# A gated delta-rule scan: the running inverse held as two stacked 64-row blocks, and decay sums turned from columns

## What is computed

```python
G = jnp.cumsum(g, axis=-1)
gamma = jnp.exp(jnp.where(incl, G[..., :, None] - G[..., None, :], -jnp.inf))
kb = k * beta[..., None]
a_low = jnp.where(strict, jnp.einsum('bhnid,bhnjd->bhnij', kb, k) * gamma, 0.0)
rhs = jnp.concatenate([v * beta[..., None], kb * jnp.exp(G)[..., None]], axis=-1)
uw = lax.linalg.triangular_solve(eye + a_low, rhs, left_side=True, lower=True, unit_diagonal=True)
qk = jnp.einsum('bhnid,bhnjd->bhnij', q, k) * gamma
...
v_new = u_n - jnp.einsum('bhck,bhkv->bhcv', w_n, s)
o_n = jnp.einsum('bhck,bhkv->bhcv', qd_n, s) + jnp.einsum('bhij,bhjv->bhiv', qk_n, v_new)
s = s * jnp.exp(gl_n)[..., None, None] + jnp.einsum('bhck,bhcv->bhkv', kd_n, v_new)
```

## Time and profile before

| | us |
|---|---|
| median of three runs | 4089.0 |
| the profiled execution's own time | 4089.51 |
| its span, first to last instruction | 4087.7 |
| TensorE matmuls busy | 3717.2 (91% of the span) |
| VectorE busy | 2009.5 (49%) |
| ScalarE busy | 910.1 (22%) |
| POOL busy | 461.1 (11%) |

### The profile page before, as it was taken

How to read it: one execution, slowest core, us unless ns; L and a number is a source line. 1 busy time by engine, 2 the same in 40 slices (tenths; PEclk the granted TensorE clock), 3 DMA queues, 4 the chain that set the end, 5 groups by cost and what they waited for, 6 DMA issues and landing times.

```text
span 4087.7 us, 54482 instructions
## 1 busy us (share of the span) xinstructions
PE 3717.2 (91%) x22980; PEld 3063.8 (75%) x22980; DVE 2009.5 (49%) x2777; ACT 910.1 (22%) x1583; POOL 461.1 (11%) x374
## 2 busy tenths in 40 slices
PE   5989999989899999898989899899999789979996
PEld 3777777767777777687878787788887667658885
DVE  3445333544453335575656566542234552765346
ACT  1114100221141001234433442110011201721011
POOL 0001000000010000004620562030000010512000
PEclk9878999988789999898999999999999989989998
DMA  3210344322103443210001003111111211012222
GB/s 131 88 56 1 142 171 178 115 94 83 52 1 142 165 171 127 108 42 13 2 27 42 13 2 122 57 55 71 63 62 62 90 62 62 1 42 93 93 93 83
DMA packets 48615, 314.44 MB, mean 77 GB/s; under 512 B 5836, under 2 KB 6732, under 8 KB 13944
## 3 DMA queue, kind: packets, MB, share of 16 engines
q1 hardware_dynamic: 37440, 272.65, 18.2%
q10 hardware_dynamic: 10936, 38.31, 2.5%
HBM read 301.38 MB, written 9.56 MB: 76 GB/s over the span
## 4 chain that ended last, share of the span: by engine, by line
PE 79%; DVE 8%; DMA 6%; issue 2%; ACT 2%; PEld 2%; POOL 1%; POOLq 0%; ACTq 0%; PEldq 0%; DVEq 0%; SPq 0%; another core or an unknown queue 0%
PE psum L511 19%; PE psum L512 18%; PE psum L513 18%; DMA pieces_in<-pieces 5%; PE psum L2072 3%; PE psum L2082 3%; PE psum L2070 2%; DVE pieces_lo L536 1%; PE psum L1127 1%; PE psum L917 1%; PE psum L1100 1%; PE psum L2902 1%; PE psum L1111 1%; PE psum L2924 1%; PE psum L1432 1%
## 5 line engine op out<-in xcount | busy, mean ns | idle before, releaser
L511 PE MATMUL psum<-xt_operands,pieces_hi 128*128 128x512 f32 (+1 forms) x2544 | 946.5, 372 | 31.0 <-DVE pieces_lo L536 26.2
L512 PE MATMUL psum<-xt_operands,pieces_hi 128*128 128x512 f32 (+1 forms) x2544 | 929.4, 365 | 0.0
L513 PE MATMUL psum<-xt_operands,pieces_lo 128*128 128x512 f32 (+1 forms) x2544 | 928.8, 365 | 0.0
L511 PEld LDWEIGHTS psum<-xt_operands,pieces_hi 128*128 128x128 f32 x2544 | 481.9, 189 | 149.5 <-issue 44.6
L529 DVE CAST pieces_hi<-pieces_in 128x2048 fp32r<-128x2048 f32 x206 | 257.3, 1249 | 576.5 <-DMA pieces_in<-pieces 490.9
L513 PEld LDWEIGHTS psum<-xt_operands,pieces_lo 128*128 128x128 f32 x2544 | 481.5, 189 | 77.8
L512 PEld LDWEIGHTS psum<-xt_operands,pieces_hi 128*128 128x128 f32 x2544 | 482.3, 190 | 75.3 <-issue 2.4
L536 DVE TENSOR_TENSOR pieces_lo<-pieces_in,pieces_hi 128x2048 fp32r<-128x2048 f32 x206 | 480.2, 2331 | 5.7
L511 PE MATMUL psum<-pieces_hi,xt_operands 128*128 128x512 f32 (+1 forms) x1000 | 403.8, 404 | 30.1 <-DVE pieces_lo L536 17.8
L512 PE MATMUL psum<-pieces_lo,xt_operands 128*128 128x512 f32 (+1 forms) x1000 | 390.8, 391 | 0.0
L513 PE MATMUL psum<-pieces_hi,xt_operands 128*128 128x512 f32 (+1 forms) x1000 | 390.7, 391 | 0.0
(11 more groups left out here) (323 smaller groups left out, 4843.2 us busy)
## 6 DMA issues: line engine op xcount, KB each, us to landing
pieces_in<-pieces SPq DMA_DIRECT2D x260, 1024.0 KB, 4.8
arena<-mods ACTq DMA_DIRECT2D x8, 512.0 KB, 14.2
arena<-ln ACTq DMA_DIRECT2D x4, 1024.0 KB, 4.8
x_park<-x_mem ACTq DMA_DIRECT2D x1, 3072.0 KB, 11.4
o_park<-arena ACTq DMA_DIRECT2D x2, 1536.0 KB, 5.4
arena<-o_park ACTq DMA_DIRECT2D x1, 3072.0 KB
x_mem<-x_park ACTq DMA_DIRECT2D x1, 3072.0 KB, 18.0
arena<-line ACTq DMA_DIRECT2D x6, 448.0 KB, 5.9
```

What stands on the lines that cost most here:

```text
L511: signal_later(k, pe.matmul(out, sh, mh, start=start, stop=False))
L512: signal_later(k, pe.matmul(out, sh, ml, start=False, stop=False))
L513: return pe.matmul(out, sl, mh, start=False, stop=stop)
```

## The change

X is no longer a 128 x 128 tile. While the inverse is built in blocks of 64 and less, only its two diagonal 64 x 64 blocks are not zero, and these are now stacked: `xc` is 128 x 64 for each head, rows 0 to 63 the upper block and rows 64 to 127 the lower one. A product with a block-diagonal stationary of 128 x 128 and `xc` as moving operand gives both blocks at once, in 64 columns (`thin`). Such a result takes 256 columns of a bank (`compact`), and VectorE adds and ScalarE copies of these are 128 x 256. The first X now comes from TensorE (`xp`, `ld` turned by a product with a stacked identity) and VectorE (`x1`). `w0` and `w1` turn the blocks by eight 64 x 64 products with an identity, `w2` by four. `v1a` places the finished blocks in a full tile `xf`, by two additions; `xf` is cleared once before the scan. `gb` becomes a transpose of the running sums, which the stage before has already put into columns (`PRE`). `ORDERS` and the loops are written out anew, and `IN_BLOCKS` names five operations, so that 10 operations of a turn use the one ring and 44 the other.

```diff
-IN_BLOCKS = ("l2", "u2", "x2", "l4", "u4", "x4", "l8", "x8", "y0", "xx0", "y1", "xx1")
+IN_BLOCKS = ("l2", "l4", "l8", "w0", "w1")
...
-def x_of(k, s, d):
-    return k.buf[d][f"x{s % 2}"]
+def compact(k, name, s, d):
+    return k.ps[:, PLACE[name, s, d][0], 0:256].rearrange("p (h c) -> p h c", c=64)
...
+    def thin(s, d, name, lhs, rhs, *needs):
 
         if not runs(s):
             return
         ready(s, d, name, needs)
-        rows, columns = halves(d)
         for h in range(HALF):
-            last = pe.matmul(bank(k, name, s, d)[rows, h, columns], lhs(s, d, h)[lhs_rows, rows],
-                             rhs(s, d, h)[lhs_rows, columns], start=True, stop=True)
+            last = pe.matmul(compact(k, name, s, d)[:, h, :], lhs(s, d, h), rhs(s, d, h), start=True, stop=True)
         st.done(last)
...
+    def turned_blocks(s, d, name, *needs):
...
+        for h in range(HALF):
+            for r in BLOCKS:
+                last = pe.matmul(bank(k, name, s, d)[r, h, r], k.buf[d]["xc"][r, h, :], k.ident[r, r], start=True, stop=True)
+        st.done(last)
...
-    def log_decay(s, d, h):
-        return g[:, CHUNKS[d][s], 4 * d + h:4 * d + h + 1].broadcast_to([P, P])
+    def prefixes(s, d, h):
+        return prefix[:, CHUNKS[d][s], 4 * d + h:4 * d + h + 1].broadcast_to([P, P])
...
     def gb(s, d):
-        product(s, d, "gb", log_decay, lambda s, d, h: tri[:, d, :])
+        product(s, d, "gb", prefixes, None)
...
+    def xp(s, d):
+        thin(s, d, "xp", b("ld"), lambda s, d, h: eye)
...
     def x2(s, d):
-        blocks(s, d, "x2", b("l2"), x, "x1")
+        thin(s, d, "x2", b("l2"), b("xc"), "x1")
...
     def w0(s, d):
-        product(s, d, "w0", x, None, "x8a")
+        turned_blocks(s, d, "w0", "x8a")
...
     def y0(s, d):
-        blocks(s, d, "y0", b("lv"), x, "lv0", "x8a")
+        thin(s, d, "y0", b("lv"), b("xc"), "lv0")
...
     def xx0(s, d):
-        blocks(s, d, "xx0", b("u2"), b("l2"), "w0c", "y0c")
+        thin(s, d, "xx0", b("u2"), b("yc"), "y0c")
...
     for d in range(2):
         e.link(dve.memset(k.state[d], 0.0))
+        e.link(dve.memset(k.buf[d]["xf"], 0.0))
...
     def v1a(s, d):
-        x = x_of(k, s, d)
-        tt(s, d, "v1a", x, ps("xx1", s, d), x, ALU.add, "xx1")
+        if runs(s):
+            st.begin("v1a", s, d, ("xx1",))
+            for r in BLOCKS:
+                ins = dve.tensor_tensor(k.buf[d]["xf"][r, :, r], compact(k, "xx1", s, d)[r, :, :],
+                                        k.buf[d]["xc"][r, :, :], ALU.add)
+            st.done(ins)
...
-    def x1(s, d):
-        tt(s, d, "x1", x_of(k, s, d), k.buf[d]["ud"], heads(k.ident), ALU.add, "ud")
```

More of the change, by code:

```diff
@@ L1538, in place2 @@
             k.buf[d][n] = room.take(HALF, P)
+        for n in ("xc", "yc"):
+            room = b if b.at + 256 <= b.end else b2 if b2.at + 256 <= b2.end else b3
+            k.buf[d][n] = room.take(HALF, 64)
     a = Arena(arena, 0, work_end)
@@ L1954 @@
 ORDERS = {
[L1955 to L1965, removed]
+    "pe": order("x4.0' l2.1' l8.0' u2.1' ks.1' x8.0' l4.1' w0.0' x2.1' y0.0' u4.1' x4.1' xx0.0' l8.1' y1.0' w1.0' "
+      "x8.1' gb.0 xx1.0' w0.1' y0.1' o1.0' xx0.1' w2.0' y2.0' w1.1' y1.1' xx2.0' gb.1 xx1.1' vn.0' o1.1' "
+      "w2.1' y2.1' o2.0' xx2.1' su.0' vn.1' kk.0 o2.1' qk.1 qk.0 kk.1 ut.0 xp.0 l2.0 ks.0 u2.0 su.1' l4.0 "
+      "x2.0 ut.1 xp.1 u4.0 "),
+    "dve": order("x2a.0' x4a.0' x1.1' x8a.0' r1.1' x2a.1' rr.1' x4a.1' v0a.0' x8a.1' diff.0 v1a.0' rr.0' v0a.1' t1.0' "
+      "s1.0' v2a.0' diff.1 v1a.1' t1.1' s1.1' v2a.1' t2.0' dlow.0 s2.0' low0.0 low.0 t2.1' qg.1 dlow.1 qg.0 "
+      "low0.1 low.1 r1.0 x1.0 s2.1' "),
+    "act": order("y1c.0' w1c.0' w0c.1' y0c.1' w2c.0' y2c.0' w1c.1' y1c.1' vnc.0' w2c.1' y2c.1' vnc.1' gam.0 gamt.0 "
+      "gamt.1 ud.0 gam.1 l2c.0 u2c.0 l4c.0 ud.1 u4c.0 l2c.1 l8c.0 u2c.1 l4c.1 w0c.0 y0c.0 u4c.1 l8c.1 "),
+    "pool": order("lv1.1' lv2.1' dup.0 kd.1' bv.1 dup.1 ld.0 oa.0' kd.0 oa.1' ld.1 lv0.0 lv0.1 lv1.0 bv.0 lv2.0 "),
 }
@@ L2080, in blocks @@
         for h in range(HALF):
-            for r in (slice(0, 64), slice(64, P)):
+            for r in BLOCKS:
                 last = pe.matmul(bank(k, name, s, d)[r, h, r], lhs(s, d, h)[r, r], rhs(s, d, h)[r, r],
                                  start=True, stop=True)
+        st.done(last)
+    def thin(s, d, name, lhs, rhs, *needs):
+        if not runs(s):
+            return
+        ready(s, d, name, needs)
+        for h in range(HALF):
+            last = pe.matmul(compact(k, name, s, d)[:, h, :], lhs(s, d, h), rhs(s, d, h), start=True, stop=True)
+        st.done(last)
+    def turned_blocks(s, d, name, *needs):
+        if not runs(s):
+            return
+        ready(s, d, name, needs)
+        for h in range(HALF):
+            for r in BLOCKS:
+                last = pe.matmul(bank(k, name, s, d)[r, h, r], k.buf[d]["xc"][r, h, :], k.ident[r, r], start=True, stop=True)
         st.done(last)
@@ L2139, in x4 @@
     def x4(s, d):
-        blocks(s, d, "x4", b("ld"), x, "x2a")
+        thin(s, d, "x4", b("ld"), b("xc"), "x2a")
     def l8(s, d):
@@ L2145, in x8 @@
     def x8(s, d):
-        blocks(s, d, "x8", b("l2"), x, "l8c", "x4a")
+        thin(s, d, "x8", b("l2"), b("xc"), "l8c")
     def w0(s, d):
-        product(s, d, "w0", x, None, "x8a")
+        turned_blocks(s, d, "w0", "x8a")
     def w1(s, d):
-        product(s, d, "w1", x, None, "v0a")
+        turned_blocks(s, d, "w1", "v0a")
     def w2(s, d):
-        product(s, d, "w2", x, None, "v1a")
+        if not runs(s):
+            return
+        ready(s, d, "w2", ("v1a",))
+        rows, _ = halves(d)
+        for h in range(HALF):
+            last = pe.matmul(bank(k, "w2", s, d)[rows, h, rows], k.buf[d]["xf"][rows, h, rows], k.ident[rows, rows],
+                             start=True, stop=True)
+        st.done(last)
     def y0(s, d):
-        blocks(s, d, "y0", b("lv"), x, "lv0", "x8a")
+        thin(s, d, "y0", b("lv"), b("xc"), "lv0")
     def y1(s, d):
-        blocks(s, d, "y1", b("lv"), x, "lv1", "v0a")
+        thin(s, d, "y1", b("lv"), b("xc"), "lv1", "v0a")
     def y2(s, d):
-        corner(s, d, "y2", b("lv"), halves(d)[1], x, "lv2")
+        corner(s, d, "y2", b("lv"), halves(d)[1], own_block, "lv2")
     def xx0(s, d):
-        blocks(s, d, "xx0", b("u2"), b("l2"), "w0c", "y0c")
+        thin(s, d, "xx0", b("u2"), b("yc"), "y0c")
     def xx1(s, d):
-        blocks(s, d, "xx1", b("u2"), b("l2"), "w1c", "y1c")
+        thin(s, d, "xx1", b("u2"), b("yc"), "w1c", "y1c")
     def xx2(s, d):
-        corner(s, d, "xx2", b("u2"), halves(d)[0], b("l2"), "w2c", "y2c")
+        corner(s, d, "xx2", b("u2"), halves(d)[0], b("yc"), "y2c")
     def ks(s, d):
@@ L2178, in vn @@
     def vn(s, d):
-        product(s, d, "vn", x, b("rr"), "v2a")
+        product(s, d, "vn", b("xf"), b("rr"), "v2a")
     def o1(s, d):
@@ L2237, in l8c, with thin_copy @@
         copy(s, d, "l8c", "l2", "l8", "l8")
+    def thin_copy(s, d, name, src, *needs):
+        if runs(s):
+            apply(s, d, name, "yc", compact(k, src, s, d), ACT.Copy, 1.0, *needs)
     def w0c(s, d):
@@ L2242, in y0c @@
     def y0c(s, d):
-        copy(s, d, "y0c", "l2", "y0", "y0")
+        thin_copy(s, d, "y0c", "y0", "y0")
     def w1c(s, d):
@@ L2299, in ps, with thin @@
         return bank(k, name, s, d) if runs(s) else None
+    def thin(name, s, d):
+        return compact(k, name, s, d) if runs(s) else None
     def col(i, s, d):
@@ L2345, in v2a @@
             st.begin("v2a", s, d, ("xx2",))
-            st.done(dve.tensor_copy(x_of(k, s, d)[rows, :, columns], bank(k, "xx2", s, d)[rows, :, columns]))
+            st.done(dve.tensor_copy(k.buf[d]["xf"][rows, :, columns], compact(k, "xx2", s, d)[rows, :, :]))
     def r1(s, d):
```

89 lines of the change are left out of this document (51 added, 38 removed).

## The result

The changed kernel takes 4167.9 us (median of 4 runs, 4162.1 to 4170.3) against 4091.0 for the kernel before (median of 4 runs, the three above and one more): a ratio of 1.018, 95% interval 1.0168 to 1.0193, so 77 us slower. The forecast was 4153 with a range of 4113 to 4177.

The account below looks back on a forecast made before the run. TensorE was taken to bound the scan. Per scan, six steps of +5.83 (35.0), +0.9 for gb, -4.0 and -1.2 for waits, +1.3 at the start make 32.0; two scans add 64 to 4089.5: 4153, range 4113 to 4177.

Parts of the forecast that it names:

- The thin product: Matmul with 128 stationary, 64 moving columns on TensorE: eight records cost 0.87 us, against 0.47 for the blocks it replaces.
- The streaming price: Rival: a thin product costs what its 64 columns stream, 0.46 us, giving 4079 us in all; chance 0.07.
- the middle price: Rival: a thin product on TensorE costs 0.65 us, giving 4113 us in all; chance 0.06.
- The waits: TensorE's waits in a turn fall from 1.9 to 1.1 us: ut.0 0.6, ks.0 0.5, qk.0's gone.
- The ring of 44: Rival: banks shared by 44 operations make new waits, 4165 or 4177 us; chance 0.11 beyond the forecast's own range.
- A steady turn: One period of the scan: TensorE's work +5.83 us, waits -0.8; the expected profile named a turn of 41.8.
- Start and end: Per scan: clearing two more tiles before the first ut.0 adds 1.3 us; longer products fill 1.2 of last-stretch waits.
- 4.57 idle, so +1.3 on the path: Scan start: TensorE idles 4.57 us before the first ut.0, so VectorE's extra clearing adds 1.3 us.
- gb: Product turned transpose on TensorE, twice a turn: 0.44 for 0.89 us, -0.90 a turn; the first turn's save nothing.

## Why the prediction was right, step by step

- **The thin product** was the main term: 0.87 from lines 1127, 1748 and 1025, measured 0.84, near the lower bound of 0.82. Three experiments show the cause: it costs 0.47 with 64 stationary columns, 0.47 as two quadrants, and 0.89 with 128 moving columns.
- **The streaming price and the middle price** fell: they were 0.46 and 0.65. The rival at 0.46 was also worked out loosely: its -0.6 a turn belongs to a price of 0.47, and by the prediction's own sum the time turns from slower to faster at about 0.52, not 0.48. The Trainium skill's shorter gap for few moving columns (TensorE: Matmul & The Clock Gate, Back-to-back issue gap) doesn't hold here, with 32-bit operands and 128 stationary columns: 0.84 for eight records is 0.105 a record.
- **The waits**: 1.1 forecast, 1.0 measured. ut.0 waits 0.6 as forecast, ks.0 0.2 where 0.5 was forecast, and a transpose waits 0.2 for ScalarE, within the limit that I had set.
- **The ring of 44** made no wait of note; the two quadrants' kernel has it and is as fast as before.
- **A steady turn**: the terms of the sum give 5.83 - 0.8 = 5.0 more, so 42.6. The text's 41.8 for a turn in its last part was a slip, and it is by luck what came, 41.82. The turn grew by 4.25, so the forecast was 0.8 too high, of which 0.5 is the thin product's 0.03 sixteen times; the other 0.3 were not traced. VectorE came to 22.80 a turn where I had 24, which changed nothing.
- **Start and end**: +1.4 measured for the clearing against 1.3. The last stretch grew by 4.7 where 6.7 - 1.2 = 5.5 was forecast.
- **The first turn** is what I missed. Two signs were there: the first ut.0, behind 4.57 of idle time, takes 1.09 where the one of a steady turn takes 0.63, and the first turn takes 38.5 where I gave all five the same 37.57 (so the last one ends at 2058.75 and not at 2057.9). But they show 0.9 us for the low clock, and not how long it would last in another kernel. The step that failed is "4.57 idle, so +1.3 on the path": it counts time lost and not the clock. It cost 6.7 a scan beyond a steady turn's share, 13 in all. Luck helped the total: this error and the opposite ones of the steady turns and the last stretch brought the sum for the scans near, 64 forecast, 68 in the profile. The time lies 15 above the forecast, by these 4, by 5 outside the scans, and by 6 by which the median lies above the profiled execution (4162.1).
- **gb** was counted at -0.9 a turn. On the kernel before that is nearly right while the clock holds (0.81); in half the turns the clock fell and took it back. In the changed kernel the steady turns read 1.00, so nothing speaks against the term there, though no run takes it out alone.

What stays open is why the clock stayed low for 18 us behind the first ut.0 in the changed kernel, and for 3 to 5 in the kernel before, with two quadrants and with twice the moving columns. TensorE was busy for 95% of those 18 us, and from 1880.85 to 1892 without a gap. The runs show which kernels do it and not by which rule.

## What to carry to other kernels

Price a matmul by its stationary columns too. With 32-bit operands and 128 stationary columns, 64 moving columns in place of 128 saved about 6% here (0.84 against 0.89), and a product of a block-diagonal matrix was cheaper as quadrants, 0.47 against 0.84. An idle stretch ahead of dense work can cost its length and then the clock behind it, so read the price of the first operations after each; here a first turn behind nearly the same stretch (4.57 and 4.46 idle) was 0.9 us longer than a steady one in the kernel before and 7.6 in the changed one. A saving on an engine that pauses in every turn may be given back to the clock. Here sixteen products in the pause, whose results nobody reads, kept it.

## What the runs showed of the hardware

Streaming twice the columns made the first turn shorter: 44.4 against 49.4 us, at a granted clock of 0.92 against 0.52 from 1875 to 1893. In the changed kernel TensorE worked from 1880.85 to 1892 without a gap, and the clock was at its lower level all that time. At the lower clock a thin product took 1.60 to 1.90 against 0.84 to 1.03, so its price follows the clock as well. And four matmuls of 64 stationary columns over all 128 rows paid 0.14 for a change of tile, going from 128 x 128 ones and going from or to 64 x 64 ones: 0.61 for the first and 0.47 for the next.
